# Row products of the adaLN modulation moved: two one step forward in u, four summed on VectorE ahead of the array, in a hybrid encoder layer with grouped experts

## The reference

```
mod = silu(c) @ w_mod + b_mod                     # 1 x 6144
sh1, sc1, g1, sh2, sc2, g2 = split(mod)           # 1024 each
h = rms_norm(x) * (1 + sc1) + sh1
u, q, k, v, g, r_f, r_b = split(h @ w_in)         # 512, 256, 256, 512, 512, 16, 16
y_pool = pool_mixer(u)            # four groups: centred mean over 2, 4, 8, 16 tokens minus the token, a 128x128 map, a scale
y_gla  = gla_mixer(q, k, v, g, r) # 4 heads, linear attention with gates, forward + strict backward, chunks of 64
x = x + g1 * (concat(y_pool, y_gla) @ w_out)
h = rms_norm(x) * (1 + sc2) + sh2
x = x + g2 * moe(h)               # sigmoid router, best of 4 groups, top 2 of its 8 experts (32 in all, 1024 -> 512 -> 1024)
out = rms_norm(x) * final_g
```

## Time and profile before

| | |
|---|---|
| median of 3 runs | 788.41 us (788.39 to 793.48) |
| profiled execution | 789.94 us, span 788.1 us |
| TensorE matmul busy | 703.7 us (89%) |
| VectorE, ScalarE, GpSimd busy | 305.3 (39%), 175.8 (22%), 46.6 (6%) |
| mean granted clock of TensorE | 0.954 of full |
| HBM read | 260.76 MB, 336 GB/s over the span |
| chain that ended last | PE 73%, DMA 17%, DVE 6%, ACT 2% |

### The profile page before, as it was taken

How to read it: one execution, slowest core, us unless ns; L and a number is a source line. 1 busy time by engine, 2 the same in 40 slices (tenths; PEclk the granted TensorE clock), 3 DMA queues, 4 the chain that set the end, 5 groups by cost and what they waited for, 6 DMA issues and landing times.

```text
span 788.1 us, 9116 instructions
## 1 busy us (share of the span) xinstructions
PE 703.7 (89%) x3786; PEld 382.2 (48%) x3786; DVE 305.3 (39%) x578; ACT 175.8 (22%) x311; POOL 46.6 (6%) x50
## 2 busy tenths in 40 slices
PE   3889999989995399999787999999999998998894
PEld 1568787457784234443333434444443443453442
DVE  3442362375786503333304233333323332322326
ACT  4323353515324011110110102101110110110104
POOL 0006600000000000000000000000000000000000
PEclk9889999999999589999996999999999999999997
DMA  9991331797027849999996899999999999999962
GB/s 333 388 382 53 107 106 66 304 387 303 10 107 300 379 162 429 423 431 397 430 404 261 323 407 430 425 427 424 426 431 425 425 427 427 426 427 426 427 283 106
DMA packets 38857, 261.23 MB, mean 331 GB/s; under 512 B 4002, under 2 KB 4386, under 8 KB 26016
## 3 DMA queue, kind: packets, MB, share of 16 engines
q1 hardware_dynamic: 34560, 250.64, 77.5%
q0 software_dynamic: 2480, 6.16, 2.0%
q10 hardware_dynamic: 1776, 3.84, 1.3%
HBM read 260.76 MB, written 4.20 MB: 336 GB/s over the span
## 4 chain that ended last, share of the span: by engine, by line
PE 73%; DMA 17%; DVE 6%; ACT 2%; issue 1%; DVEq 0%; SPq 0%; POOLq 0%
PE bank L854 24%; PE bank L585 18%; DMA ring<-in_w 12%; PE bank L863 12%; PE bank L871 3%; PE bank L872 2%; DMA x_rows<-mid 2%; PE bank L537 2%; PE bank L828 2%; PE bank L843 1%; DVE x L1593 1%; DMA xg_rows<-x_rows,keep 1%; DMA after<-in_b_mod 1%; PE bank L846 1%; PE bank L711 1%
## 5 line engine op out<-in xcount | busy, mean ns | idle before, releaser
L854 PE MATMUL bank<-ring,low 128*64 128x512 f32 x1024 | 230.7, 604 | 14.0 <-DMA ring<-in_w 11.3
L854 PEld LDWEIGHTS bank<-ring,low 128*64 128x64 f32 x1024 | 77.8, 139 | 157.0 <-issue 157.0
L1593 DVE TENSOR_TENSOR x<-x,bank 128x512 f32<-128x512 f32 x136 | 84.4, 681 | 84.8 <-PE bank L872 83.0
L863 PE MATMUL bank<-ring,low 128*64 128x512 f32 x512 | 113.4, 595 | 1.0 <-DVE x L1593 0.9
L863 PEld LDWEIGHTS bank<-ring,low 128*64 128x64 f32 x512 | 36.2, 137 | 66.1 <-issue 64.5
L1583 DVE SCALAR_TENSOR_TENSOR y_raw<-bank,keep,g2b 128x512 f32<-128x512 f32 x32 | 24.0, 751 | 88.5 <-PE bank L863 88.5
L1643 DVE TENSOR_TENSOR low<-low,bank 128x512 f32<-128x512 f32 x16 | 11.0, 688 | 115.4 <-PE bank L854 115.4
L871 PE MATMUL bank<-y_hi,slot_tok 128*128 128x512 f32 x128 | 53.7, 420 | 0.2 <-DVE y_lo L1588 0.2
L872 PE MATMUL bank<-y_lo,slot_tok 128*128 128x512 f32 x128 | 50.5, 394 | 0.0
L1255 ACT COPY low<-bank 128x512 f32<-128x512 f32 x16 | 9.4, 586 | 177.2 <-PE bank L836 177.2
L585 PE MATMUL bank<-h_hi,w_hi 128*128 128x512 f32 x96 | 40.3, 419 | 6.2 <-DVE w_lo L1331 3.3
(11 more groups left out here) (246 smaller groups left out, 809.3 us busy)
## 6 DMA issues: line engine op xcount, KB each, us to landing
ring<-in_w SPq DMA_DIRECT2D x99, 2048.0 KB, 21.4
ring<-in_w_mod SPq DMA_DIRECT2D x12, 2048.0 KB, 14.9
ring<-in_w_in SPq DMA_DIRECT2D x4, 2048.0 KB, 17.7
ring<-in_w_out SPq DMA_DIRECT2D x2, 2048.0 KB, 12.8
x<-in_x SPq DMA_DIRECT2D x4, 512.0 KB, 6.0
after<-in_b_mod POOLq DMA_DIRECT2D x1, 2048.0 KB, 7.7
x_rows<-mid ACTq DMA_DIRECT2D x4, 512.0 KB, 11.4
out<-x SPq DMA_DIRECT2D x4, 512.0 KB, 2.6
```

Source lines behind the costliest of these rows:

```text
L854: last = mm(bk[e * CAP:(e + 1) * CAP, :], xb[:, k, e * CAP:(e + 1) * CAP], unit(n % SLOTS, KD)[:, k, :], start=k == 0, stop=k == KD - 1)
L863: last = mm(bk[e * CAP:(e + 1) * CAP, :], hid_t[:, k, e * CAP:(e + 1) * CAP], unit(n % SLOTS, KF)[:, k, hf * 512:(hf + 1) * 512], start=k ...
L1593: return v.tensor_tensor(acc[:, t, c], acc[:, t, c], bk[:, :], ALU.add)
```

## The change

1. In u's hook, rows 1, columns 1 with rows 3, and columns 3 stand one k step earlier (ahead of steps 1, 2, 3). xT7's transposes go behind columns 2, and its copy on VectorE behind the first low part.
2. m4 goes to a ninth place, MIDDLE (the tile `mid`, free once xT7 is made), and is loaded between qk and v. m4 to m7 are no longer multiplied on the array with c as the stationary operand: VectorE adds up, in place and for each partition, w[k] * cs[k] over k in the halves of g1b and sh2b (`mod_steps`, eight operations for each of four blocks), spread between the low parts 8 to 31. One product with ones then sums over the partitions and spreads (jobs mb4 to mb7, right behind g), and VectorE copies the result.
3. The bias of g1 and sh2 is loaded into row 0 of the cleared sums (two loads of 4 KB, POOL's queue, at the start), that of sc2 into sc2b (0.5 MB broadcast, behind the pooling windows), that of g2 as one row behind g. The load of 2 MB is gone.
4. Behind g: mb4 to mb7, then pair 8, then the attention. mrow has four places. m5 to m11 have other slots, and the first two expert units change places.

```diff
+        + [f"mb{i}" for i in range(4, 8)] + [f"m{a}{8 + j}" for a in "rb" for j in range(2)]
...
-STREAM = dict(m0=0, m2=1, u=2, m1=3, m3=0, qk=1, v=3, g=0, m4=2, m5=1, m6=3, m7=0, m8=2, m9=1, m10=3, m11=0, wo0=2, wo1=1)
+MIDDLE = SLOTS
+STREAM = dict(m0=0, m2=1, u=2, m1=3, m3=0, qk=1, m4=MIDDLE, v=3, g=0, m5=2, m6=1, m7=3, m8=2, m9=1, m10=0, m11=3,
+              wo0=2, wo1=1)
+SUMMED = [f"m{i}" for i in range(4, 8)]
...
+            elif name in SUMMED:
+                eng.wait_ge(mod_summed, KD * (SUMMED.index(name) + 1))
...
+                elif slot == MIDDLE:
+                    sp.wait_ge(job_done, JOB["xT7"] + 1)
...
-            for n in (3, 0, 2, 1, 4, 5, 6, 7):
+            for n in (0, 3, 2, 1, 4, 5, 6, 7):
...
-                if k == 2:
+                if k == 1:
                     mod_rows(1, later_rows[1])
-                elif k == 3:
+                elif k == 2:
                     mod_columns(later_columns, 1)
                     mod_rows(3, later_rows[3])
-                elif k == 4:
+                elif k == 3:
                     mod_columns(later_columns, 3).then_inc(job_done, 1)
...
-            mod_pair(4)
-            mod_pair(6)
+            pe.wait_ge(tmp_in, 16)
+            for i in range(4):
+                b = start(f"mb{i + 4}")
+                pe.wait_ge(mod_summed, KD * (i + 1))
+                mm(b[:, :], ones, mod_sum[i], start=True, stop=True).then_inc(job_done, 1)
+            mod_pair(8)
...
+            act.wait_ge(mod_summed, KD)
             for i in range(4):
                 b = full(act, f"gk{i}")
...
             for i in range(4):
                 decays(i)
-                mod_part(4 + i)
+                if i < 2:
+                    mod_part(8 + i)
...
+            def mod_steps(n0, n1):
+
+                for n in range(n0, n1):
+                    i, k = divmod(n, KD)
+                    slot = STREAM[SUMMED[i]]
+                    if k == 0:
+                        dve.wait_ge(landed[slot], 16 * arrival(SUMMED[i]))
+                        dve.wait_ge(bias_rows_in, 32)
+                    else:
+                        dve.wait_ge(mod_summed, n)
+                    v.scalar_tensor_tensor(mod_sum[i], unit(slot, KD)[:, k, :], cs[:, k:k + 1], mod_sum[i],
+                                           ALU.mult, ALU.add).then_inc(mod_summed, 1)
+
+            def low_weights_and_mods(c0, c1):
+
+                for c in range(c0, c1):
+                    low_weights(c, c + 1)
+                    if c < 2 * KD:
+                        mod_steps(c - KD, c - KD + 1)
+                    else:
+                        mod_steps(KD + (c - 2 * KD) * 3 // 2, KD + (c + 1 - 2 * KD) * 3 // 2)
+
+            low_weights_and_mods(8, 20)
...
-            low_weights(24, 28)
+            low_weights_and_mods(24, 28)
             for t in range(NT):
                 b = full(dve, f"v{t}")
                 v.tensor_copy(v_s[:, t, :], b[:, :]).then_inc(out_vector, 1)
-            low_weights(28, 32)
+            low_weights_and_mods(28, 32)
...
-            dve.wait_ge(bias_in, 16)
+            for i in range(4, 8):
+                mod_row(i)
             decayed(0)
             decayed(1)
-            mod_row(4)
-            mod_row(5)
+            dve.wait_ge(bias_in, 16)
+            mod_row(8)
+            mod_row(9)
             decayed(2)
             decayed(3)
-            mod_row(6)
-            mod_row(7)
...
+            link(g_.memset(spread[:, :], 0.0))
+            for i, z in enumerate((g1b, sh2b)):
+                pool.dma_start(z[0:1, :], A["b_mod"][:, (2 + i) * D:(3 + i) * D]).then_inc(bias_rows_in, 16)
...
+            pool.wait_ge(wr_parts, 1)
...
+            pool.dma_start(sc2b, A["b_mod"][:, 4 * D:5 * D].to_broadcast([P, D])).then_inc(bias_in, 16)
             pool.wait_ge(job_done, JOB["g3"] + 1)
-            pool.dma_start(bias_b, A["b_mod"][:, 2 * D:6 * D].to_broadcast([P, 4 * D])).then_inc(bias_in, 16)
+            pool.dma_start(g2bias, A["b_mod"][:, 5 * D:6 * D]).then_inc(g2bias_in, 16)
```

More of the change, by code:

```diff
@@ L116, in constants @@
     return cp, np.concatenate([ct, ce], 1), cm, i8
-JOBS = ([f"xT{k}" for k in range(4)] + ["mr0", "xT4", "xT5", "mr2", "xT6", "xT7", "mcol0", "mr1", "mr3", "mcol1"]
+JOBS = ([f"xT{k}" for k in range(4)] + ["mr0", "xT4", "xT5", "mr2", "xT6", "mcol0", "xT7", "mr1", "mr3", "mcol1"]
         + [f"u{i}" for i in range(4)] + ["r", "q0", "q1", "k0", "k1"] + [f"gk{i}" for i in range(4)]
         + [f"v{i}" for i in range(4)] + [f"yp{i}" for i in range(4)] + [f"g{i}" for i in range(4)]
-        + [f"m{a}{i + j}" for i in (4, 6) for a in "rb" for j in range(2)]
+        + [f"mb{i}" for i in range(4, 8)] + [f"m{a}{8 + j}" for a in "rb" for j in range(2)]
         + [f"att{d}{h}" for d in range(2) for h in range(HEADS)]
         + [f"kdt{d}{p}" for d in range(2) for p in range(2)]
-        + [f"m{a}{8 + j}" for a in "rb" for j in range(2)]
         + [f"upd{d}{p}{par}" for d in range(2) for p in range(2) for par in range(2)]
@@ L151 @@
               + [f"yp{i}" for i in range(4)] + [f"g{i}" for i in range(4)]
-              + [f"mr{i}" for i in range(4, 8)]
+              + ["mr8", "mr9"]
               + [f"kdt{d}{p}" for d in range(2) for p in range(2)]
-              + [f"mr{i}" for i in range(8, 12)] + [f"o{h}" for h in range(HEADS)]
+              + ["mr10", "mr11"] + [f"o{h}" for h in range(HEADS)]
               + [f"hT{t}{hf}" for t in range(NT) for hf in range(2)] + ["lg"])
-OUT_VECTOR = ([f"xT{k}" for k in range(KD)] + ["mcol0", "mcol1"] + [f"v{i}" for i in range(4)] + [f"mb{i}" for i in range(4, 8)]
-              + [f"att{d}{h}" for d in range(2) for h in range(HEADS)] + ["mb8", "mb9"]
+OUT_VECTOR = ([f"xT{k}" for k in range(7)] + ["mcol0", "xT7", "mcol1"] + [f"v{i}" for i in range(4)] + [f"mb{i}" for i in range(4, 10)]
+              + [f"att{d}{h}" for d in range(2) for h in range(HEADS)]
               + [f"upd{d}{p}{par}" for d in range(2) for p in range(2) for par in range(2)]
@@ L211, in build @@
         spread = place("spread", YA, [P, 3 * D])
-        wr_raw = spread[:, D:2 * D]
         g1b, sc2b, sh2b = (spread[:, i * D:(i + 1) * D] for i in range(3))
@@ L232, in build @@
         after = place("after", 4 * UNIT, [P, 2 * UNIT])
-        mrow = after[:, 0:1024].rearrange("p (a n) -> p a n", a=2)
-        g2row = after[0:1, 1024:2048]
-        bias_b = after[:, UNIT:2 * UNIT]
+        mrow = after[:, 0:2048].rearrange("p (a n) -> p a n", a=4)
+        g2row, g2bias = after[0:1, 2048:3072], after[0:1, 3072:4096]
         sq = after[:, UNIT + 2048:2 * UNIT].rearrange("p (h t) -> p h t", h=HEADS)
@@ L279, in build @@
         base += CT_N + EDGE_N
-        ta, tb = spread[:, 2 * D:2 * D + 528], scr[:, base:base + 528]
+        tb, ta = scr[:, base:base + 528], scr[:, base + 528:base + 1056]
         rst = tb[:, 0:512]
-        base += 528
+        wr_raw = scr[:, base:base + D]
+        base += 1056
+        mod_sum = [z[:, i * 512:(i + 1) * 512] for z in (g1b, sh2b) for i in range(2)]
         base = (base + 15) // 16 * 16
@@ L332, in sems @@
             return [sem(n) for n in names.split()]
-        landed = [sem(f"landed{i}") for i in range(SLOTS)]
+        landed = [sem(f"landed{i}") for i in range(SLOTS)] + [sem("landed_middle")]
         x_in = [sem(f"x_in{t}") for t in range(NT)]
-        cols_in, ident_in, keep_in, tmp_in, small_in, wr_in, bias_in = sems(
-            "cols_in ident_in keep_in tmp_in small_in wr_in bias_in")
+        cols_in, ident_in, keep_in, tmp_in, small_in, wr_in, bias_rows_in, bias_in, g2bias_in, mod_summed = sems(
+            "cols_in ident_in keep_in tmp_in small_in wr_in bias_rows_in bias_in g2bias_in mod_summed")
         job_done, out_scalar, out_vector = sems("job_done out_scalar out_vector")
@@ L371, in unit @@
         def unit(slot, k):
+            if slot == MIDDLE:
+                return mid.rearrange("p (k n) -> p k n", k=k)
             return ring[:, slot, :].rearrange("p (k n) -> p k n", k=k)
@@ L560, in _ @@
             mod_rows(2)
-            banks = [start("xT6"), start("xT7")]
+            before_last = start("xT6")
             columns = start("mcol0")
             mod_columns(columns, 0)
-            x_transposed(6, banks[0])
-            x_transposed(7, banks[1])
+            x_transposed(6, before_last)
             mod_columns(columns, 2).then_inc(job_done, 1)
+            x_transposed(7, start("xT7"))
             later_rows = {i: start(f"mr{i}") for i in (1, 3)}
@@ L647, in mod_pair @@
                     read_out(pe, f"mr{j}")
-                    mm(b[:, :], sel, mrow[:, j % 2, :], start=True, stop=True).then_inc(job_done, 1)
-            mod_pair(4)
-            mod_pair(6)
+                    mm(b[:, :], sel, mrow[:, j - 8, :], start=True, stop=True).then_inc(job_done, 1)
+            pe.wait_ge(tmp_in, 16)
[4 more added lines that the diff above has]
+            mod_pair(8)
             for d in range(2):
@@ L671, in _ @@
```

(38 more changed lines are left out.)

7 lines of the change are left out of this document (3 added, 4 removed).

## The result

The changed kernel takes 780.87 us (median of 4 runs, 778.89 to 784.04) where the kernel before takes 788.85 in the same comparison. The medians differ by 8.0 us; the ratio over all these runs is 0.9891, 95% interval [0.9868, 0.9913], which makes 8.6 us less, between 6.9 and 10.4. Forecast were 778.8 and a range of 775.5 to 783.5. The profiled execution has a span of 777.0 us and a time of 778.89; it is the fastest of the four.

A forecast was written before the change was run, and what follows sets the result against it. The expert stage was taken as held by its weight stream, which waits on the front, a chain mostly of TensorE. 5.2 + 9.2 - 2.5 - 2.3 = 9.6 us off the median of 788.41 gave 778.8 us, range 775.5 to 783.5.

The forecast's parts named there:

- Part 1: In u, late row products one step earlier: 5.2 us gained, 2.3 by step 4's start, 2.9 by the clock.
- Part 2: Sums on VectorE: a new stop of 2.5 us ahead of g, 2.3 more for the clock, 4.8 us lost.
- Part 3: Stretch after g: masks 2.9 us earlier, mod_pair(8) off the path, state recurrences 9.2 us earlier; bounds 8 to 9.5.
- The pass through the experts: From the front to the end: what comes off the front comes off the end, one for one.
- The signs of being wrong: Sums at twice their price near the scans, half clock at other places, or a last stage of changed length.
- (a): At g the clock does not fall, 2.3 us more gain: 776.5 us; chance 0.22.
- (b): u keeps its slow stretch, so the move there gives 2.3 us alone: 781.7 us; chance 0.12.
- (c): Stretch after g gives less, copies of mr8 and mr9 delay decays; 3 us lost: 781.8 us; chance 0.17.
- (d): VectorE becomes the bound around the scans, slower than before; 790.6 us at 1.6 us a sum; chance 0.03.
- (e): The front shrinks but the expert stream ends where it did: 788 us; chance 0.04.

The follow-up runs named there:

- part1_alone: The kernel before with only u's late row products and columns one k step earlier: 786.27 us, ratio 0.9953 to the kernel before.
- part1_undone: The whole change with u's row products and columns put back ahead of steps 2, 3 and 4: 785.76 us, ratio 0.9944 to the kernel before.
- decays_first: The whole change with six sums behind the copies of v, and ScalarE's decays(1) ahead of its copies of mr8 and mr9: 774.44 us, ratio 0.9810.
- v_first: The whole change with the six sums behind low parts 24 to 27 moved behind the copies of v: 775.58 us, ratio 0.9831 to the kernel before.
- bias_later: The kernel before with VectorE's wait for the 2 MB bias load moved from ahead of decayed(0) to behind decayed(1): 787.24 us, ratio 0.9964.
- pair8_back: The whole change with mod_pair(8), its copies and its mod rows back behind the kdt transposes: 781.95 us, ratio 0.9899 to the kernel before.
- twice_sums: The whole change with each of the 32 sums made as two operations with half the factor: 792.80 us, ratio 1.0036 to the kernel before.

## Why the prediction was right

**Part 1, forecast 5.2, measured 5.83** (2.98 by the start, 2.85 by the clock). That both come from this edit is shown from either side (part1_alone 5.0 in u, part1_undone 4.1 in u); the start is worth 2.2 to 3.0 in these pairs, and the half clock behind the same stop 1.6 to 2.9. The wait of 0.5 us for m3 did not occur: m3 was issued at 18.0 and landed 20.4 later, at 38.4, just ahead of its use at 38.63. The landing was between 38.0 (decays_first) and 39.3 (before) in the profiles, so this term was finer than one trace can carry. Step 0 did start earlier, by 0.91 us, but it ran longer at half clock and ended only 0.09 earlier (33.05 against 33.14), so that it counts 0 was right. The clock stayed at 1.00, as taken.

**Part 2, forecast a loss of 4.8, measured 5.1.** The mechanism is shown by v_first. The stop was 3.27 us and not 2.5: I priced a sum by the spacing of L1359's four (0.62), but with a column as factor a sum takes 0.745 (median), 0.78 from start to start where one waits for the other, so six cost 4.2 us. The slack ahead of g was also 1.0 us and not 1.2, since g's product starts 0.83 us behind the start of the first copy. The clock fell, for 1.83 us of cost where I had 2.3. Beside POOL's windows the sums took 1.1 to 1.3 us on average, as the one row of before had it (1.22). By the Trainium skill (SBUF — State Buffer, "SBUF: two separate sides"), VectorE operations with two inputs from SBUF and GpSimd operations that read SBUF shut each other out for a whole instruction. The trace agrees: away from the windows, from 92 us on, every sum took 0.74 or 0.75. In the change as it is this cost nothing; with twice the sums it cost 3 us at g.

**Part 3, forecast 9.2, measured 8.64** (9.37 at the recurrence less 0.73 at g's end). 3.4 of it had come by the masks, and bias_later shows that much for the wait for the bias alone; 5.2 lie between masks and recurrence, where pair 8 had stood. The masks came 15.4 us behind g's end (said: 16), the first recurrence 21.6 behind it (said: 21). VectorE waited for ScalarE's decays(1), which stood behind mr8, for 1.03 us, as laid out. What was undersized is the clock: upd's first products took 1.67 us instead of 1.11, half of what the lower bound of 8 allowed for. The 3.44 us that I took for kdt was itself a row at half clock (the kernel before had 0.50 from 163 to 165, behind a stop of 2.65 us that the prediction does not name); at full clock kdt took 2.08 to 2.54. pair8_back shows that I could have had most of the gain with the pair in its old place: with the full clock, its 5.5 us cost net 1.3.

**The pass through the experts** held in direction (v_first's 5.6 us at o became 4.7 in the ratio, twice_sums' 11.9 became 11.4). The spread of 1 to 2 us is that of the last stage, 510.8 to 513.8 us long in the profiles; what moves it is open.

**The signs of being wrong** that the prediction names did show in part: the half clock came at other places (within the attention products from 155.7, in the router from 237.6), and the last stage was 1.8 us shorter. The first cost 0.6 us of part 3 and nothing in the router by the time of the gathered rows; the second is within the spread. So the forecast holds by its parts 1 to 3, but that the clock's falls cost so little elsewhere was not foreseen.

**The rivals.** (a) did not come: the clock fell at g. (b) fell with the granted clock of 1.00 behind 47.3. (c) came in small, 0.6 us, by the clock and by mr8. (d) was priced at a turning point of 1.4 us for each sum; twice_sums, at 1.5, is slower than before, by 0.36%. (e) fell. The sum of the front, 9.6 forecast and 9.37 measured, hides errors of +0.6, -0.3 and -0.6 that cancelled; that it comes so close is luck. That the clock falls at g was a choice between two values, and the stop of 2.72 us in the router, followed by half clock in some profiles and not in others, shows that it could have gone the other way. Of the chances, faster by over 1% is what the median says, with an interval that reaches over that line.

## What to carry to other kernels

When filler work is given to an engine with free time, don't price it against the average: look for the one place where the engine is late already and something of another engine's waits behind it in the queue. Here 26 of 32 sums cost nothing and six cost 5.1 us, and moving these six behind four copies gave them back. And when a stall goes, try the edit that only moves the wait: four changed lines in the old kernel gave 7.3 us, where the whole change gave 8.6.

## What the runs showed of the hardware

A stop of TensorE of 3.27 us was followed by about 3.5 us at 1.2 GHz, as the one of 2.93 us in u was by 5.9 us. But the length of a stop does not decide it. The same stop of 2.72 us in the router left the clock at 1.00 in the changed kernel, in the kernel before and in decays_first, and was followed by half clock in v_first, pair8_back and twice_sums; TensorE's timeline of the changed kernel, then of v_first:

```profile
235.89 1.09 PE L793 MATMUL bank<-keep,mid 128*128 128x128 f32 x8 [2.72 <-DVE mid L1529]
```

```profile
230.23 1.74 PE L793 MATMUL bank<-keep,mid 128*128 128x128 f32 x8 [2.72 <-DVE mid L1530]
```

More of a surprise: the stretch with the attention products had the half clock in two profiles with this order (kdt 3.67 us, and 3.44 in decays_first) and not in others (2.54 in v_first, 2.52 in twice_sums and part1_undone), though the stops ahead of its fall are short in all of them: 0.79 and 0.77 us in the changed kernel, and at most the 1.37 ahead of kdt in decays_first, which v_first, twice_sums and part1_undone have too. And v had the half clock for about 3 us in decays_first and part1_undone with no stop at all. With one profile for each kernel, whether the order or the execution decides is open. In the attention stretch it is worth 1 to 1.7 us. An in-place scalar_tensor_tensor of 128x512 with a column as factor took 0.745 us, against 0.68 with a constant.
